# First four output tiles of W_O in Strassen's block form, and S3 loaded third in both stages of that form

## The reference, cut to what matters

```python
merged = jax.nn.sigmoid(g_a) * (o_a @ w_a) + jax.nn.sigmoid(g_b) * (o_b @ w_b)
return x + merged @ w_o, S_new, conv_new, h_last
```

## Time and profile before

| | us |
|---|---|
| median of 3 runs | 1903.36 (1902.87 to 1903.52) |
| the profiled execution | 1904.28 |
| its span in the profile | 1902.4 |
| PE busy | 1879.9 (99%), 12984 matmuls |
| DVE busy | 1262.3 (66%) |
| ACT busy | 805.4 (42%) |
| POOL busy | 284.4 (15%) |

### The profile page before, as it was taken

One profiled execution on the slowest core, in us unless ns is written; L12 is line 12 of the kernel. 1 busy time (PEld: TensorE's weight loads), 2 busy tenths in 40 slices (PEclk: granted clock), 3 DMA queues, 4 the chain that ended last, 5 costly groups with the idle time before them and its releaser, 6 DMA issues.

```text
span 1902.4 us, 32236 instructions
## 1 busy us (share of the span) xinstructions
PE 1879.9 (99%) x12984; PEld 1762.1 (93%) x12984; DVE 1262.3 (66%) x2144; ACT 805.4 (42%) x1293; POOL 284.4 (15%) x399
## 2 busy tenths in 40 slices
PE   8999999999999999999999999999999999999998
PEld 7899898898899999999998988988988999999997
DVE  8775665665766877864487656657557678878445
ACT  5432332423437776542344323234124377766323
POOL 2220120120232200100022201202102422001000
PEclk9999999999999999999999999999999999999999
DMA  6434544453443432643354445534544533327332
GB/s 219 134 120 165 168 140 131 161 183 110 144 157 91 112 99 91 157 121 115 104 173 157 141 126 177 172 114 150 167 120 144 165 101 107 98 83 193 103 122 78
DMA packets 114786, 257.48 MB, mean 135 GB/s; under 512 B 11822, under 2 KB 52254, under 8 KB 114510
## 3 DMA queue, kind: packets, MB, share of 16 engines
q1 hardware_dynamic: 84350, 156.00, 26.4%
q0 software_dynamic: 30144, 99.41, 16.6%
q10 hardware_dynamic: 144, 0.00, 0.0%
HBM read 196.55 MB, written 49.12 MB: 129 GB/s over the span
## 4 chain that ended last, share of the span: by engine, by line
PE 86%; DVE 5%; ACT 3%; DMA 2%; DVEq 1%; issue 1%; ACTq 1%; SPq 0%
PE bank L1944 20%; PE bank L1946 20%; PE bank L1945 20%; PE bank L2014 4%; PE bank L2015 4%; PE bank L2016 4%; DMA w_raw<-in_w_units 1%; PE last L2032 1%; PE last L2014 1%; PE last L2016 1%; PE last L2015 1%; PE bank L2282 1%; PE bank L2285 1%; PE bank L2284 1%; PE sums L2147 1%
## 5 line engine op out<-in xcount | busy, mean ns | idle before, releaser
L1944 PE MATMUL bank<-xn_hi,w_hi 128*128 128x296 f32 (+1 forms) x2176 | 651.9, 300 | 0.4 <-DVE w_lo L531 0.2
L1946 PE MATMUL bank<-xn_lo,w_hi 128*128 128x296 f32 (+1 forms) x2176 | 647.6, 298 | 0.0
L1945 PE MATMUL bank<-xn_hi,w_lo 128*128 128x296 f32 (+1 forms) x2176 | 646.8, 297 | 0.0
L1944 PEld LDWEIGHTS bank<-xn_hi,w_hi 128*128 128x128 f32 x2176 | 409.9, 188 | 6.9 <-issue 4.3
L1945 PEld LDWEIGHTS bank<-xn_hi,w_lo 128*128 128x128 f32 x2176 | 410.5, 189 | 1.0
L1946 PEld LDWEIGHTS bank<-xn_lo,w_hi 128*128 128x128 f32 x2176 | 409.5, 188 | 0.0
L524 ACT ACTIVATE w_hi<-w_raw 128x1024 fp32r<-128x1024 f32 x229 | 240.7, 1055 | 357.8 <-DMA w_raw<-in_w_units 355.3
L531 DVE TENSOR_TENSOR w_lo<-w_raw,w_hi 128x1024 fp32r<-128x1024 f32 x229 | 280.6, 1228 | 93.3 <-ACT w_hi L524 86.5
L1944 PE MATMUL bank<-oa_hi,w_hi 128*128 128x296 f32 (+1 forms) x512 | 154.0, 301 | 0.0
L1945 PE MATMUL bank<-oa_hi,w_lo 128*128 128x296 f32 (+1 forms) x512 | 152.1, 297 | 0.0
L1946 PE MATMUL bank<-oa_lo,w_hi 128*128 128x296 f32 (+1 forms) x512 | 152.0, 297 | 0.0
(11 more groups left out here) (331 smaller groups left out, 3540.9 us busy)
## 6 DMA issues: line engine op xcount, KB each, us to landing
w_raw<-in_w_units SPq DMA_DIRECT2D x199, 512.0 KB, 3.7
S<-in_state_ret POOLq DMA_DIRECT2D x64, 512.0 KB, 4.8
out_ret_s<-S POOLq DMA_DIRECT2D x64, 512.0 KB, 6.2
w_raw<-in_w_units SPq DMA_DIRECT2D x122, 256.0 KB, 3.2
vst<-v_scr SPq DMA_DIRECT2D x8, 512.0 KB, 4.1
out_ret_p<-Sp POOLq DMA_DIRECT2D x8, 512.0 KB, 5.7
w_raw<-in_w_units POOLq DMA_DIRECT2D x16, 256.0 KB, 4.8
v_scr<-vtok_hi SPq DMA_DIRECT2D x16, 160.0 KB
```

What stands on the lines that cost most here:

```text
L1944: pe.matmul(ps, w_hi[:, slot, cols], x_hi, start=first, stop=False)
L1945: pe.matmul(ps, w_lo[:, slot, cols], x_hi, start=False, stop=False)
L1946: return pe.matmul(ps, w_hi[:, slot, cols], x_lo, start=False, stop=last)
```

## The change

Four of the eight output tiles of W_O are now made as two more pairs in block form (pairs 4 and 5 of a layer), and four by plain projection, with x of the first four taken straight from the banks. What was kept by copies in the gate stage is here added to x as it comes: DVE's `taken` adds a bank to one tile and one part of the rows, with a factor of 0.5 or -0.5, and counts `x_taken`; PE waits for it where a product adds to a bank whose former sum has to be out. The right sides are made per tile of `merged` (`of_merged`) during W_B. The last tile of W_B runs its first four blocks for both parts of the rows first. In both stages of block form, S3 is loaded as third part; the order of the products stays. The places of the ring are now worked out by a table (`ring_places`), and each load waits for what held its place eight earlier. POOL reloads x in pairs of tiles k and k+4. The diff, cut to its core. The order of the loads and the places of the ring, then SP and POOL:

```diff
+LOAD_ORDER = (A11, S1, S3, S2, A12, S4, A22)
...
+            for first, pairs in ((B_AT, range(TILE_PAIRS)), (O_AT, range(TILE_PAIRS, LAYER_PAIRS))):
+                if at == first:
+                    for two in pairs:
+                        for part in LOAD_ORDER:
+                            n = (l * LAYER_PAIRS + two) * PRODUCTS + part
+                            part_at[n] = len(held)
+                            held.append(("part", n + 1))
+            unit_at.append(len(held))
+            held += [("unit", len(unit_at))] * 2
+    return held, unit_at, part_at
...
+            def wait_room(place):
+
+                kind, count = HELD[place - PART_RING]
+                sp.wait_ge(unit_done if kind == "unit" else part_done, count)
+
+            def load_parts(l, pairs):
+
+                for two in pairs:
+                    for part in LOAD_ORDER:
+                        n, (m, k) = two * PRODUCTS + part, PART_FROM[part]
+                        wait_room(PART_PLACE[l * PART_UNITS + n])
+                        sp.dma_start(part_of(w_raw, l, n), w_units[stored_pair(l, two) + m]
...
+
+                    pool.wait_ge(mgl_ready, l * KT + k + 5)
+                    apart(pool)
+                    for m in (k, k + 4):
+                        pool.dma_start(acc[:, m, :], (x_in if l == 0 else x_scr[l - 1])[:, m * T:m * T + T])\
+                            .then_inc(x_again[k], 16)
+
+                    add_part(two, S1)
+                    add_part(two, S3)
+                load_again(0)
+                add_part(TILE_PAIRS, S1)
+                load_again(1)
+                load_again(2)
+                add_part(TILE_PAIRS, S3)
+                load_again(3)
+                for two in range(TILE_PAIRS + 1, LAYER_PAIRS):
+                    add_part(two, S1)
+                    add_part(two, S3)
```

ACT, in the loop over the tiles of W_B and behind it:

```diff
+                    elif done == 10:
+                        part_high(TILE_PAIRS, S1)
+                        part_high(TILE_PAIRS, S2)
+                        part_high(TILE_PAIRS, A12)
...
+                    if m < 4:
+                        merged_high(m)
+                        of_merged_high(m + 1, diff_hi, diff, m)
+                    else:
+                        k = m - 4
+                        if m < KT - 1:
+                            merged_high(m)
+                        of_merged_high(4 + 3 * k + 2, mix2_hi, mix2, k)
+                        if m == KT - 1:
+                            merged_high(m)
+                        of_merged_high(4 + 3 * k + 2, edge_hi, edge, k)
+                        of_merged_high(4 + 3 * k + 3, last_hi, last_right, k)
...
+                two = TILE_PAIRS
+                part_high(two, S3)
+                part_high(two, S4)
+                part_high(two, A22)
+                part_high(two + 1, A11)
+                part_high(two + 1, S1)
+                part_high(two + 1, S2)
+                part_high(two + 1, A12)
+                two += 1
+                part_high(two, S3)
+                part_high(two, S4)
+                part_high(two, A22)
+                tile_high(0)
+                split_hi(act, "O", l, 0, 0 - AHEAD)
+                tile_high(1)
+                split_hi(act, "O", l, 0, 1 - AHEAD)
+                split_hi(act, "O", l, 0, 2 - AHEAD)
+                tile_high(2)
+                tile_high(3)
```

DVE, ahead of and in the loop over the tiles of W_B, and behind it:

```diff
+                    elif done == 10:
+                        part_add(TILE_PAIRS, S2, S1)
+                        part_low(TILE_PAIRS, S1)
+                        part_add(TILE_PAIRS, S4, S2)
+                        part_low(TILE_PAIRS, S2)
...
+                    if m < 4:
+                        dve.tensor_tensor(diff[:, m, 0:wide], acc[:, m, a0:b0], acc[:, m, a1:b1], SUB).then_inc(right_ready, 1)
+                        return
+                    k = m - 4
+                    dve.tensor_tensor(edge[:, k, 0:wide], acc[:, m, a1:b1], acc[:, k, a1:b1], SUB).then_inc(right_ready, 1)
+                    dve.drain()
+                    dve.scalar_tensor_tensor(mix2[:, k, 0:wide], acc[:, k, a0:b0], -1.0, edge[:, k, 0:wide], MUL, SUB)\
+                       .then_inc(right_ready, 1)
+                    dve.drain()
+                    dve.scalar_tensor_tensor(last_right[:, k, 0:wide], mix2[:, k, 0:wide], -1.0, acc[:, m, a0:b0], MUL, SUB)\
+                       .then_inc(right_ready, 1)
...
+                    dve.drain()
+                    of_merged(m)
                     if m >= 1:
                         low_merged(m - 1)
+                        if m <= 4:
+                            of_merged_low(m, m - 1)
+                        else:
+                            for part in range(3):
+                                of_merged_low(5 + 3 * (m - 5) + part, m - 5)
+                    if m % 2 == 0:
+                        next_low(done)
...
+                    a, b = cut(l)[part]
+                    if first_of is not None:
+                        dve.wait_ge(x_again[tile % 4], l * 32 + 32)
+                    dve.wait_ge(part_done, l * PART_UNITS + two * PRODUCTS + product + 1)
+                    dve.scalar_tensor_tensor(acc[:, tile, a:b], ps[:, 0:wide], scale, acc[:, tile, a:b], MUL, ADD)\
+                       .then_inc(x_taken, 1)
+                    dve.drain()
+                    if last_of:
+                        dve.sem_inc(x_ready, 1)
...
+                two, x = TILE_PAIRS, bank[0]
+                of_merged_low(4 + 3 * 3 + 1, 3)
+                taken(two, A11, x, 0, 0, 0.5, True)
+                part_low(two, A12)
+                low_merged(KT - 1)
+                taken(two, S1, bank[2], 1, 1, -0.5, True)
+                of_merged_low(4 + 3 * 3 + 2, 3)
+                taken(two, S2, x, 0, 1, 0.5)
+                part_low(two, S3)
+                of_merged_low(4 + 3 * 3 + 3, 3)
+                taken(two, A12, bank[3], 0, 0, 0.5)
+                part_low(two, S4)
+                part_low(two, A22)
+                taken(two, S3, x, 1, 1, -0.5)
+                part_low(two + 1, A11)
+                taken(two, S4, bank[2], 0, 1, 0.5, None, True)
+                part_add(two + 1, S2, S1)
+                part_low(two + 1, S1)
+                taken(two, A22, x, 1, 0, -0.5, None, True)
+                part_add(two + 1, S4, S2)
+                part_low(two + 1, S2)
+                two, x = two + 1, bank[1]
+                taken(two, A11, x, 2, 0, 0.5, True)
+                part_low(two, A12)
+                taken(two, S1, bank[2], 3, 1, -0.5, True)
+                tile_low(0)
+                taken(two, S2, x, 2, 1, 0.5)
+                part_low(two, S3)
+                part_low(two, S4)
+                taken(two, A12, bank[3], 2, 0, 0.5)
+                part_low(two, A22)
+                taken(two, S3, x, 3, 1, -0.5)
+                split_lo(dve, "O", l, 0, 0 - AHEAD)
+                taken(two, S4, bank[2], 2, 1, 0.5, None, True)
+                split_lo(dve, "O", l, 0, 1 - AHEAD)
+                taken(two, A22, x, 3, 0, -0.5, None, True)
+                tile_low(1)
+                split_lo(dve, "O", l, 0, 2 - AHEAD)
+
```

PE, at the end of W_B and in the output stage:

```diff
+                        if early:
+                            if n == 1:
+                                ins.then_inc(unit_done, 1)
+                        elif early is False and n == 1:
+                            ins.then_inc(unit_done, 1)
+                        else:
+                            done("B", name, ins)
+                at = l * RIGHTS + 4
+                for t in range(OUT_PAIRS):
+                    two, before, x, y, z = TILE_PAIRS + t, (l * OUT_PAIRS + t) * PRODUCTS, bank[t], bank[2], bank[3]
+                    x, y, z = x[:, 0:wide], y[:, 0:wide], z[:, 0:wide]
+                    wait_bank(pe, "O", l, 0, (("proj", 0), t))
+                    product(two, A11, x, xn_hi[:, 0:4, a0:b0], xn_lo[:, 0:4, a0:b0], True,
+                            mgl_ready, l * KT + 1, 1)
+                    if t == 0:
+                        wait_bank(pe, "O", l, 0, (("proj", 1), 0))
+                    else:
+                        pe.wait_ge(x_taken, before - PRODUCTS + S4 + 1)
+                    product(two, S1, y, diff_hi[:, :, 0:wide], diff_lo[:, :, 0:wide], True, right_lo, at + 1, 1)
+                    pe.wait_ge(x_taken, before + A11 + 1)
+                    product(two, S2, x, mix2_hi[:, :, 0:wide], mix2_lo[:, :, 0:wide], False, right_lo, at + 5, 3)
+                    if t == 0:
+                        wait_bank(pe, "O", l, 0, (("proj", 1), 1))
+                    else:
+                        pe.wait_ge(x_taken, before - PRODUCTS + A12 + 1)
+                    product(two, A12, z, xn_hi[:, 4:KT, a0:b0], xn_lo[:, 4:KT, a0:b0], True, mgl_ready, l * KT + 5, 1)
+                    pe.wait_ge(x_taken, before + S2 + 1)
+                    product(two, S3, x, edge_hi[:, :, 0:wide], edge_lo[:, :, 0:wide], False, right_lo, at + 6, 3)
+                    pe.wait_ge(x_taken, before + S1 + 1)
```

(67 more changed lines are left out.)

199 lines of the change are left out of this document (91 added, 108 removed).

## The result

The changed kernel takes **1923.03 us** (median of 4 runs, 1920.94 to 1924.24) against 1903.11 before on the same chip: ratio 1.0102, interval 1.009 to 1.0115, 19.9 us slower. Its profiled execution took 1920.94 (span 1918.8, granted clock 0.997), the quickest of the four.

A forecast was written before the change was run, and what follows sets the result against it. PE was taken to bound the kernel, busy for 99% of the span with 86% of the chain. Terms -6.5-3.1+7.3+5.3+5.6+2.2+1.3 = +12.1 us on the median of 1903.4 gave 1915.5, range 1903 to 1925.

The forecast's parts named there:

- Part 1: Output stages: two pairs of seven products take 168 matmuls for 192 a layer; -6.5 us for both layers.
- Part 2: Gate-stage load order: earlier S3 loads remove four waits, -3.1 us; later S2 loads add waits before S1, +7.3.
- Part 3: Output stage start: PE waits before S2 until DVE's list reaches the taking of A11; +5.3 us.
- Part 4: First output pair: S3 waits for its accumulate, queued behind load_again(2) on POOL; +5.6 us.
- Part 5: Second output pair: S1 waits for S2's load, S2 starts late behind DVE's list; +2.2 us for both layers.
- Part 6: End of layer 1: unit 3 of W_O is split late, behind DVE and ACT backlog; +1.3 us.
- (a): Rival: DVE's list and accumulates keep up, all waits go, faster at 1893.8 us; chance 0.13.
- (b): Rival: quick landings only, gate stage clean, the wait for DVE's taking stays; no change at 1902.8 us; chance 0.17.
- (c): Rival: clock falls to 1.2 GHz behind four new waits of 2.6 us and more; 1922 us; chance 0.05.

The follow-up runs named there:

- experiment 11: Kernel of experiment 9 with x reloads split by tile: 2 and 3 early, 6 and 7 behind S3's accumulate of the second output pair; 1902.94 us, ratio 1.0004.
- experiment 2: Changed kernel with the old load order in the gate stage alone, S3 third only in the output stage; 1914.1 us, ratio 1.0061.
- experiment 6: Changed kernel with old load order in both stages, S3's accumulate ahead of load_again(2), and the taking of A11 early; 1910.17 us, ratio 1.0036.
- experiment 5: Changed kernel with the old load order in both stages of block form; 1911.24 us, ratio 1.0042.
- experiment 3: Changed kernel with S3's accumulate for the first output pair ahead of load_again(2) on POOL; 1920.19 us, ratio 1.0094.
- experiment 4: Changed kernel with DVE's taking of A11 right behind the second sum of tile 7, low half of tile 6 later; 1928.08 us, ratio 1.0138.
- experiment 10: Kernel of experiment 9 with the last reload of x behind S3's accumulate of the second output pair; 1915.05 us, ratio 1.0049.
- experiment 7: Kernel of experiment 6 with S3 loaded as fourth part in the gate stage; 1915.87 us, ratio 1.0068.
- experiment 9: Kernel of experiment 6 with S1's accumulate of pair 5 ahead of load_again(2) and DVE's low halves and takings reordered; 1905.48 us, ratio 1.0015.
- experiment 1: Kernel before with only the new gate-stage load order, S3 third, and no block form in the output stage; 1912.65 us, ratio 1.0051.

## Why the prediction was right, and where it was not

The forecast was slower, 1915.5 in 1903 to 1925; it is slower, 1923.0. The mechanisms were largely the ones named; the size was 7.5 us short.

- **Part 1** (-6.5): right. 48 matmuls fewer. Even experiment 11, with the shortest waits, keeps only 0.8 of the 6.5 in the two output stages.
- **Part 2** (-3.1 and +7.3): this is the step that failed, a term of the sum mis-sized. The net was put at +4.2. Against the profile before, the gate stages measure +6.0 and the first W_B tiles +2.0; against experiment 2, +7.9 and +1.9; by medians the order costs 10.2 alone and 8.9 in company.
  - The waits before S1 came (1.5 and 0.5 for pairs 1 and 3 in layer 0; 1.1, 0.3 and 0.5 in layer 1), but they make 3.9, not 7.3. S2 landed after 2.9 to 4.8 us, 3.7 on average, where the step took 4.2.
  - What it put at nothing outweighed that. The bunch that it named itself (S2, with A12 and S4 behind it) landed after 4.2, 6.8 and 7.0 us for pair 1 of layer 1, and S4, not S2, was last: 2.0 us of waits before S2. The waits for S3 shrank from 2.9 to 1.8 rather than went.
  - It also left out the ring's far end: a unit of W_B waits for the place in which S3 now stands, and the halves of ob are queued behind those units' on ACT and DVE, 2 us in the stage after.
  - The -3.1 may be too much in itself: with the old order in the changed kernel the waits before products come to 1.0 in both gate stages (experiment 2).
- **Part 3** (+5.3): right as a sum of row times: taking 5.3 us behind the start as worked out, S2 at 5.83 and 5.73 for 5.9, waits 2.42 and 2.39 for 2.6 and 2.7.
- **Part 4** (+5.6): the start of S3 was right, 12.10 and 11.98 for 11.9, and so was the way (landing 5.1 and 5.0 for 4.8). Its wait of 1.2 and 1.5 is smaller than the 2.7 only because the lower clock had used up the difference. The Trainium skill, "SBUF — State Buffer", section "SBUF: two separate sides", would have put this accumulate at the long end, beside a full DVE list; it landed after 5.1, so the trace does not bear that out. One did take 7.7 (8.3 in layer 1) where four reloads went out just ahead of it (experiment 6).
- **Part 5** (+2.2): right in the sum. Pair 5 ends at 29.5 us of the stage, forecast 29.4; three waits of about 0.5 (S2 in both layers, S1 in layer 1).
- **Part 6** (+1.3): measured 1.7 from the end of pair 5 on, so the size was near; the cause was one that part 5 had put at 0. It is the load order of the output stage: with the old order there the 1.7 is gone (36.95 in experiment 5, against 38.68), though the square sums and results stand on DVE in the same order. SP sent unit 1 of W_O 3.0 us ahead of the plain tiles, where experiment 5 has 6.2: the ring's far end again. DVE waited 2.6 us for its high half, with the last taking, the square sums and the result of tile 4 behind it, and PE waited 0.8 for that result. The split of unit 3 was not what it waited for.

```profile
1881.88 1.23 DVE L561 TENSOR_TENSOR w_lo<-w_raw,w_hi 128x1024 fp32r<-128x1024 f32 x1 [2.60 <-ACT w_hi L554]
...
1885.66 1.61 DVE L1335 TENSOR_TENSOR sqs<-sqs,sq 128x576 f32<-128x576 f32 x2
1887.19 0.45 DVE L2084 SCALAR_TENSOR_TENSOR acc<-bank,acc 128x288 f32<-128x288 f32 x1
```

- **Rivals.** (a), that all keeps up, fell on the list it named. (b), quick landings, fell on the bunched loads. (c), the clock falls, had 0.05 and came true in part: it had four falls, and there was one in each layer, with the first new wait of 2.4 us. The price of 1.6 for the product is what experiment 3 lays bare; in the changed kernel's profiled execution the wait for S3 hides it. The Trainium skill, "TensorE: Matmul & The Clock Gate", section "HAM oscillation — how this bites in real kernels", has waits for DMA throttle PE again. The trace agrees as far as it goes: here waits of 2.4 us for DVE did, and waits up to 1.8 did not. The chance was too small: a wait longer than any seen is no ground for taking the clock as it was.
- **The profiled execution.** It is 16.7 slower than the one before; the median is 19.9 slower. The other three runs of the changed kernel (1922.0, 1924.0, 1924.2) had a mean granted clock of 0.996, 0.995 and 0.995 against 0.997. That they lost more to the clock is likely, but no profile of them shows where.

## What to carry to other kernels

Saving matmuls pays only if each engine's in-order list keeps up with the shorter stage: write down, per list, when each product's last input is due, and set bulk transfers that nobody needs soon (here x of tiles 6 and 7) behind the accumulates. Moving one load ahead in a ring moves others back; follow the last of them through every operation queued behind its consumer, and into the next stage. Take the cost of a stage from a kernel that differs in this one thing, and from more than one profile: here the one profile of the kernel before had a stage 1.9 us longer than its like. And a new wait longer than any in the trace may cost more than itself: with 12 of 13 waits of 2.4 to 3.3 us the clock fell.

## What the hardware showed that was not expected

- **The clock and the length of a wait.** Over all these profiles, of 13 waits of 2.4 to 3.3 us inside a layer's block form, 12 came with a stretch at 1.2 GHz at or behind their end, 3.4 us long in each (the thirteenth, of 2.7, is in experiment 4); with the four longest, 3.7 to 7.2 us (experiments 4 and 10), it was 6.8. None followed waits up to 1.8; of three between 2.0 and 2.3 us one did (2.03, experiment 5) and two did not (2.07, experiment 3; 2.27, experiment 7). A fall cost 1.6 us in experiment 3, and nothing in the changed kernel, where the next product was late anyway.
- **Transfers beside each other.** A load of 256 KB has a median of 3.2 us. Sent within some 2 us of reloads of x it took 6.7 to 6.9 with four of them (experiment 9) and 5.8 to 7.1 with two (experiment 10). In layer 0 of experiment 11 one sent 1.1 us behind a single reload took 3.0, and the next, 0.7 behind an accumulate, 4.7.
- **Reordering the loads** in a ring of eight cost half a per cent by itself (experiment 1), with the same bytes and as many matmuls.
